# A decoder layer in one kernel: two groups of tiles become three

## What is computed

```python
n = rmsnorm(x, norm1_w)
qa, ka, va, qb, fb, ib, gb, ga, gbr = split(n @ w_in)        # 512 * 7 + 1024 * 2 columns
oa = diff_attn(qa, ka, va, lam)                  # 4 heads, two softmax maps each, causal
ob = hgrn2(silu(qb), lb + (1 - lb) * sigmoid(fb), ib) * silu(gb)   # 4 heads, a 128x128 state each
h = x + (sigmoid(ga) * (oa @ w_branch_a) + sigmoid(gbr) * (ob @ w_branch_b)) @ w_out
# PEER: 8 heads pick 16 of 16384 experts each, 128 per token
q = rmsnorm(h, norm2_w) @ w_query
idx, w = top16_of_sums(top16(q1 @ keys1), top16(q2 @ keys2)), softmax(...)
h = h + sum_s w[s] * gelu(n2 . expert_u[idx[s]]) * expert_v[idx[s]]
y = rmsnorm(h, norm_f_w)
```

## Time and profile before

| | |
|---|---|
| runs, median | 4544.08 us (4537.21 to 4554.89) |
| profiled execution, span | 4543.0 us (the page gives no other time of it) |
| PE, busy | 2851.9 us, 63% |
| DVE, busy | 2761.8 us, 61% |
| POOL, busy | 1419.0 us, 31% |
| ACT, busy | 770.2 us, 17% |
| moved by DMA | 1245.86 MB, 274 GB/s over the span |
| of it by gathers and other indirect DMAs | 1098.98 MB |
| TensorE's mean granted clock | 0.799 |

### The profile page before, as it was taken

One profiled execution on the slowest core, in us unless ns is written; L12 is line 12 of the kernel. 1 busy time (PEld: TensorE's weight loads), 2 busy tenths in 40 slices (PEclk: granted clock), 3 DMA queues, 4 the chain that ended last, 5 costly groups with the idle time before them and its releaser, 6 DMA issues. The chain is left out here.

```text
span 4543.0 us, 27167 instructions
## 1 busy us (share of the span) xinstructions
PE 2851.9 (63%) x7469; PEld 1351.7 (30%) x7469; DVE 2761.8 (61%) x5875; ACT 770.2 (17%) x1942; POOL 1419.0 (31%) x1130
## 2 busy tenths in 40 slices
PE   6964696529722322322286676787777777778777
PEld 3432233217211110011175232332233233222222
DVE  1044114966479989799656457557646755755673
ACT  1035101101134421244233000000010000001000
POOL 0000000014345557544223234333333333342441
PEclk9976798759866655655588898988899889888987
DMA  5201422049779888988687988889989988987995
GB/s 178 84 26 32 153 75 73 10 161 349 260 305 357 343 306 324 364 314 324 223 315 314 376 344 342 339 339 353 351 320 352 367 331 341 354 343 312 348 350 216
DMA packets 228998, 1245.86 MB, mean 274 GB/s; under 512 B 26040, under 2 KB 56376, under 8 KB 95104
## 3 DMA queue, kind: packets, MB, share of 16 engines
q0 software_dynamic: 153728, 1098.98, 62.7%
q1 hardware_dynamic: 75136, 145.37, 8.9%
HBM read 1210.87 MB, written 33.39 MB: 274 GB/s over the span
## 5 line engine op out<-in xcount | busy, mean ns | idle before, releaser
L2073 PE MATMUL x_acc<-arena 128*128 128x512 f32 x2560 | 1334.6, 676 | 531.7 <-DVE arena L2176 531.4
L2184 DVE CUSTOM_DVE_ANT_0 arena<-arena 128x1024 f32<-128x1024 f32 x640 | 777.2, 1222 | 736.6 <-DMA arena<-in_experts,arena 727.1
L2025 POOL DMA_INDIRECT arena<-in_experts,arena x648 | 751.7, 1160 | 1250.5 <-PE x_acc L2073 1087.5
L1485 POOL DMA_INDIRECT arena<-in_experts,arena x384 | 594.5, 1548 | 1752.3 <-POOLq L163 969.0
L2073 PEld LDWEIGHTS x_acc<-arena 128*128 128x128 f32 x2560 | 531.9, 216 | 1321.2 <-DVE arena L2176 709.3
L1522 DVE SCALAR_TENSOR_TENSOR arena<-arena 128x1024 f32<-128x1024 f32 x384 | 491.3, 1280 | 127.6 <-ACT arena L1500 127.4
L1556 DVE CUSTOM_DVE_ANT_0 arena<-arena 128x1024 f32<-128x1024 f32 x384 | 467.6, 1218 | 36.4 <-DMA arena<-in_experts,arena 34.7
L2138 ACT ACTIVATE arena<-arena 128x2 f32<-128x2 f32 x320 | 65.1, 203 | 1765.0 <-DVE arena L2184 1764.9
L2176 DVE TENSOR_SCALAR arena<-ident,arena 128x128 f32<-128x128 f32 x640 | 191.2, 341 | 0.0
L476 PE MATMUL ptb<-arena 128*128 128x260 f32 x512 | 116.4, 387 | 97.2 <-DMA arena<-in_w_t 97.1
L1498 ACT ACTIVATE arena<-arena 128x1 f32<-128x1 f32 x384 | 77.3, 201 | 547.8 <-DVE arena L1556 526.4
(11 more groups left out here) (365 smaller groups left out, 3102.3 us busy)
## 6 DMA issues: line engine op xcount, KB each, us to landing
arena<-in_w_t SPq DMA_DIRECT2D x64, 512.0 KB
arena<-in_experts,arena POOLq DMA_INDIRECT x1032
arena<-in_w_n SPq DMA_DIRECT2D x6, 2048.0 KB, 12.1
arena<-in_w_out SPq DMA_DIRECT2D x2, 4096.0 KB, 12.9
arena<-in_w_query SPq DMA_DIRECT2D x2, 4096.0 KB
arena<-xnt_scratch SPq DMA_DIRECT2D x2, 2080.0 KB
arena<-in_x SPq DMA_DIRECT2D x4, 1024.0 KB
xnt_scratch<-arena SPq DMA_DIRECT2D x8, 512.0 KB, 4.2
```

Source lines behind the costliest of these rows:

```text
L1485: pool.indirect_dma_start(out=c["ring"][:, s0 % RING, :], out_offset=None, in_=self.io["experts"], in_offset=bass.IndirectOffsetOnAxis(ap= ...
L2025: nc.gpsimd.indirect_dma_start(out=ring[:, r, :], out_offset=None, in_=io["experts"], in_offset=bass.IndirectOffsetOnAxis(ap=rows_at, axis ...
L2073: last = nc.tensor.matmul(acc[:, n * 512:(n + 1) * 512], diag[:, s % RING, :], ring[:, s % RING, D + n * 512:D + (n + 1) * 512], start=(s ...
L2184: ins = v.tensor_tensor_reduce(out=ring[:, r, 0:D], in0=ring[:, r, 0:D], in1=n2_cur[:], scale=1.0, scalar=0.0, op0=ALU.mult, op1=ALU.add, ...
```

## The change

`GROUPS`, the list of tile ranges, gets a third entry. All code that depends on it follows: the slices' widths, the tiles of each `Side`, which tile is handed over, the stages' loops.

```diff
-GROUPS = ((0, 4), (4, NT))
+GROUPS = ((0, 2), (2, 5), (5, NT))
```

## The result

The kernel with three groups takes 4605.95 us (median of 4 runs, 4597.25 to 4619.42), the one before 4549.49 us beside it on the same chip: ratio 1.0127, 95% interval 1.0101 to 1.0152. The profiled execution's span is 4602.2 us, 59 above the 4543.0 of before.

What follows compares the result with a forecast made beforehand. Gathers and VectorE's work on them were taken to bound the kernel from 976 on, the group's own work before. Group A gives back 246, experts 395; fronts cost 134 more, B and C 674: net +167, 4710 us, range 4620 to 4785.

Steps and rivals of the forecast that it cites:

- The sign and its mechanism: Whole kernel: slower (0.92), net +167 us, as the extra group repeats weight passes, stage heads and a stretch without gathers.
- experts 1671: Experts stage: one turn of the loop fewer, 2066 − 395 = 1671 us.
- the fronts 433: Fronts after groups A and B: 181 and 252 us, together 433 for 299, 134 more.
- group A with normalise 431: Normalise untouched at 43 us, group A's two tiles without slots 388 us instead of 634.
- At 350 GB/s, between rows 1 and what the earlier trace lets stand, 113 MB are 324 us: Project B: bound by transfers, 113 MB take 324 us, plus 11 for the stage's end: 335 us.
- The merges: Merge B 212 us with chunks of 22 us for late weights; merge C 172 us with chunks of 17.5.
- HGRN B and C: HGRN stages of groups B and C: own work, slots and idle make 191 and 205 us.
- The sample stage: Samples in group C: 19 slots fewer at 2.34 us each, 231 us down to 188.
- The sum with 435: Total at the fabric's 435 GB/s: project B 260 + 11, merge B some 30 shorter, about 4615 us; not used.
- The slots fill the gaps: Rival, groups B and C: extra slots lie in VectorE's idle time, B and C 1908 us, total 4442; chance 0.03.
- Cost by tiles: Rival, groups B and C: a group's cost goes by its tiles, 53 us each, total 4537; chance 0.05.
- Weights starve: Rival, project B and merges: slots hold weight loads back further, 35 + 31 + 30 us more, total 4805; chance 0.12.

Runs made afterwards that it cites:

- experiment 3: Three groups of tiles 0, 1-3 and 4-8, slots beside and experts tiles as in the two-group kernel, against that kernel: 4704.17 us, ratio 1.0339.
- Experiment 1: Two-group kernel with 15, 30 or 46 slots moved from attention to project in the last group: ratios 0.994, 0.9907 and 0.988.
- Experiment 2: Slots left out beside group b of the two-group kernel and beside group B of the three-group kernel: those groups alone take 943.3 and 543.0 us.
- experiment 4: Three-group kernel with two row-weight buffers in every group (N_BESIDE 2 instead of 3): 4585.15 us, ratio 1.0074 to the kernel before.
- experiment 7: Two-group kernel, project share 30, more slots moved from attention to merge: attention 15, 11, then 15 with merge share 17; ratios 0.9865, 0.9856, 0.9846.
- 30/19: Two-group kernel with shares 30 for project and 19 for attention in the last group, 46 slots moved between them: ratio 0.988.

## Why the prediction was half right

*The sign and its mechanism held.* A group has a price of its own, experiment 3 puts it at 150 us (134 without the 16 that its experts stage came out longer), and what the tile taken from the experts stage brings, net of its slots beside a group, is less. The terms read from single rows came out close: experts 1671 for 1664.5, the fronts 433 for 428.1, attention 222 and 268 for 222.0 and 266.9, project C 262 for 261.4, group A with normalise 431 for 415.7. The first gather came at 594.4, where 612 was named.

*The step that failed* is "At 350 GB/s, between rows 1 and what the earlier trace rows lets stand, 113 MB are 324 us". The bytes were right: 288.5 us at 393 GB/s are 113 MB. The rate was not: it stood at 421 and 422 GB/s in the two windows of 40 us above. The mistake was one of reading. The earlier trace rows were taken as "transfers are the limit", while the same row has TensorE busy 47.96 of 50 us at the full clock. Experiment 1 shows that this window took 80 GB/s more when it was given more slots. The prediction's own scaling of the earlier trace rows to a full share gave 366 and 392, and it used up to 391 for the merge chunk; at 391 project B would have been 300. Of the 108 us between the forecast's 4710 and the span of 4602, 46 lie in project B. The term is the largest but not the whole: with it right the forecast would have been 4664, still 62 above the span. The rest are a dozen small terms of which one alone, the samples, was too short. Why the others lean one way was not looked for.

*The merges* were 9 and 10 too long, and not by the rate. In merge B the first two chunks went at 18.4 and 15.5 us from start to start, without a wait, where the forecast gave every chunk the 22 of a late weight load. The five behind them took 22.3 in the mean, as forecast. In merge C most chunks took TensorE's own 15.8 us, with one wait of 1.7 behind the first, and not 17.5.

*Smaller terms.* Group A and normalise were 15 too dear, mostly in the estimates of short blocks (project A 128 for 122.4) and of HGRN. HGRN B and C were taken with the idle time of group b's, which has one more tile a head: 11 and 7 too long (idle 30 and 34.5 for the 39 and 41 assumed). The sample stage went the other way, 197.5 for 188: with 19 slots fewer beside it, it got shorter by 1.8 us for each and not by 2.34. Experiment 2 has 1.3 for a slot there in the mean, so some of the slots lie in time that the stage needs anyway. The experts stage took 1664.5 us here and 1674.3 to 1683.0 in the traces of the other three-group kernels with four tiles in it, with the same code, so the 6 us by which 1671 missed it carry no weight. One reading was off without a price: group a's HGRN stands at a granted clock of 0.70 in the earlier trace rows, outside the prediction's 0.54 to 0.63.

*The two rules of the Trainium skill.* The prediction weighed the ceiling of "DMA: Bandwidth & Descriptors" in the Trainium skill, section Specifications, and set it aside, since "the trace has stayed on the side of the lower figure". That was misread: the second of the earlier trace rows has 372 GB/s over 50 us, above 358, and the stretch from 1254 has 398. These runs show 420 to 423 GB/s in stretches of 50 us, near the page's fabric figure of 435 and above its 358. The sum with 435 was about 4615, 10 us from what was measured, but that nearness is in part luck: it had project B at 271, where 288.5 were measured, and merge B 30 shorter, at 182, where 203 were measured, and these two errors made up for the terms that were too long. Merge A has 384 passes in 86.9 us, 0.23 each at half the width of the 0.43. So width is paid in proportion here too, and the rule weighed from "TensorE: Matmul & The Clock Gate" in the Trainium skill, section Back-to-back issue gap, would have moved the sum further away, to 4780.

*The rivals.* "The slots fill the gaps" was given 0.03 and a total of 4442. As a total it is wrong, as a mechanism it was a good part of the truth: slots cost 1.5 us beside a group and not 2.34, and the point that was to decide it, 400 GB/s in project B's columns, was passed. It failed as a whole because attention and HGRN, where VectorE sets the pace, leave few gaps (1.7 to 2.0 us a slot), and because the group's own 543 us stay. "Cost by tiles" fell in experiment 3. "Weights starve" came in part. In the groups of instructions of the kernel after (busy us, mean ns; then the idle time before them and what ended it) TensorE's idle time before merge B's weights is 52 us, and 110 before those of project B's columns:

```profile
L1374 PE MATMUL b_mg_ps<-arena 128*128 128x384 f32 x256 | 98.2, 543 | 52.0 <-DMA arena<-in_wb 52.0
...
L476 PE MATMUL ptb<-arena 128*128 128x384 f32 x256 | 94.9, 528 | 110.0 <-DMA arena<-in_w_t 109.9
```

Both sums hold idle time from before the stage began. Of the 110, 82 end at the first block of columns, and TensorE had been idle since fronts A's last matmul, at 527, while the stage began at 593.5: within it are 16 us at the head and 28 between blocks. Within merge B they are 16 at the head and 25 between chunks, where merge b has 2, and the forecast had already put 7 × (22 − 15.6) = 45 there. The gathers ran on in these waits, so they may cost the stage less than their length; that was tried only for the row weights (experiment 4). Merge B came out 9 below the forecast, not above it.

*The chances.* The forecast's own range, 4640 to 4775, rested on one value of project B's rate, and its low end did not hold the case of a higher one, though the prediction had priced it.

## What to carry to other kernels

A DMA share of 0.93 beside an engine that is itself busy all the time did not show that the transfers were the limit. Look for a stretch in which no engine is busy all the time and take the rate from there; a stage is bound by its bytes only if it gets longer by what the added bytes take at that rate. Background work should be dealt out by its price in each stage, and leaving it out once measures that: in the two-group kernel 0.25 to 0.9 us a slot beside matmuls and 1.9 beside VectorE's own work, so moving 46 of 384 slots from attention to project brought 1.2%. But this is the mean price of the slots that are there: merge took 47 at 0.25 each and asked 1.6 to 2.2 for each of the next 16 (experiment 7), so the price of more has to be measured by adding some. Cutting work into more groups pays each group's weights, heads and unaccompanied stages again, here 150 us net, so it must earn more than that elsewhere.

## What the runs showed of the hardware

- In float32 loads and gathers of 8 KB rows, the 16 DMA engines together moved 420 to 423 GB/s over windows of 50 us (30/19, from 1050, 1150 and 1200), with 4 KB-row weight loads among them; the busy share then reads 1.01 to 1.02. A share of 0.93 went with 340 in one window and with 380 in another, 0.95 with 372, 1.00 with 398: the share says little on how much room is left.
- Matmul passes in float32 are paid by their width. In stretches of the merges without a wait and at a granted clock of 1.00, the same 24 passes come again every 10.32 us at 512 columns (merge a of the kernel before, 516.88 to 527.20), 7.90 at 392 and 7.74 at 384 (merges C and B of the changed kernel), and 5.26 at 260 (merge b): 0.43, 0.33, 0.32 and 0.22 us a pass. Averages over whole stages are higher where the clock was lower, 0.36 at 384 columns in merge B with 0.83.
- The experts stage, the same code in all kernels with five tiles in it, took between 2060.8 and 2082.4 us in the profiled executions, and 1664.5 to 1683.0 in the three-group kernels with four. What makes these 1% was not looked for; differences below it in a single trace were given no weight.
